# A two-block transformer kernel: second projection's chunks in another order, the gate's turn later, and splits, turns and squares moved at the handovers

## The reference

```python
# first block
h = rms_norm(x, g)
proj = h @ w_in            # 8708 columns: q, k, v of four kinds of attention, forget logits, gates
x = x + sum(sigmoid(gate) * (ys @ w_branch)) @ w_out
h = rms_norm(x, g)
x = x + square(relu(h @ w_up)) @ w_down          # 4096 hidden
x = rms_norm(x, g)
# second block
h = rms_norm_2(x, g)
q, k, v, u = split(h @ w_in)                     # 512 + 512 + 512 + 1024 columns
q, k = rope(rms_norm(q)), rope(rms_norm(k))      # by head of 64
attn = moba_attention(q, k, v)
a, g = split(u + b)
conv = silu(layer_norm(depthwise_conv31(a * sigmoid(g)) + b))
x = x + concat(attn, conv) @ w_out
h = rms_norm_2(x, g)
x = x + (silu(h @ w_gate) * (h @ w_up)) @ w_down # 2816 hidden
```

## Time and profile before

| | us |
|---|---|
| three timed runs | 823.29, 818.70, 821.35 (median 821.35) |
| the profiled execution | 819.01 |
| its span | 817.2 |
| PE busy | 784.6 |
| DVE busy | 476.5 |
| ACT busy | 407.1 |
| POOL busy | 41.7 |

### The profile page before, as it was taken

One profiled execution on the slowest core, in us unless ns is written; L12 is line 12 of the kernel. 1 busy time (PEld: TensorE's weight loads), 2 busy tenths in 40 slices (PEclk: granted clock), 3 DMA queues, 4 the chain that ended last, 5 costly groups with the idle time before them and its releaser, 6 DMA issues.

```text
span 817.2 us, 9727 instructions
## 1 busy us (share of the span) xinstructions
PE 784.6 (96%) x3930; PEld 657.3 (80%) x3930; DVE 476.5 (58%) x623; ACT 407.1 (50%) x542; POOL 41.7 (5%) x38
## 2 busy tenths in 40 slices
PE   7999999999999899999999999898999999999997
PEld 5787889888888687888888877776887888888896
DVE  5555365657765867454445437788956644545443
ACT  6565455455656536455454545555455543343340
POOL 0200000000000400000000004011000000000000
PEclk9999999999999999999999999999999999999999
DMA  9842424434445355655655553845122755655341
GB/s 330 312 156 81 152 78 156 154 114 145 155 157 203 117 183 198 212 182 176 205 185 176 196 165 132 332 147 168 53 63 96 255 192 172 203 177 184 104 155 51
DMA packets 68508, 136.25 MB, mean 167 GB/s; under 512 B 2416, under 2 KB 7152, under 8 KB 67824
## 3 DMA queue, kind: packets, MB, share of 16 engines
q1 hardware_dynamic: 68000, 134.44, 48.3%
q10 hardware_dynamic: 464, 1.20, 0.4%
HBM read 134.43 MB, written 1.05 MB: 166 GB/s over the span
## 4 chain that ended last, share of the span: by engine, by line
PE 80%; DVE 10%; ACT 5%; issue 3%; POOL 1%; DMA 1%; ACTq 0%; SPq 0%; DVEq 0%; POOLq 0%
PE b L573 18%; PE b L575 18%; PE b L574 18%; PE SS L573 4%; PE SS L574 4%; PE SS L575 4%; PE TT L542 3%; DVE ca L1913 2%; DVE wlo L1457 2%; PE OO L575 2%; PE OO L574 2%; PE OO L573 2%; ACT whi L1035 2%; PE SS L656 1%; PE b L713 1%
## 5 line engine op out<-in xcount | busy, mean ns | idle before, releaser
L1457 DVE TENSOR_TENSOR wlo<-raw,whi 128x2048 fp32r<-128x2048 f32 (+2 forms) x123 | 273.9, 2229 | 165.0 <-ACT whi L1035 164.8
L1035 ACT CAST whi<-raw 128x2048 fp32r<-128x2048 f32 (+2 forms) x123 | 227.3, 1850 | 125.4 <-PE b L575 87.5
L573 PE MATMUL b<-whi,Ahi 128*128 128x512 f32 (+2 forms) x568 | 222.1, 391 | 4.3 <-DVE wlo L1457 1.8
L575 PE MATMUL b<-whi,Alo 128*128 128x512 f32 (+2 forms) x568 | 215.4, 379 | 0.0
L574 PE MATMUL b<-wlo,Ahi 128*128 128x512 f32 (+2 forms) x568 | 214.9, 378 | 0.0
L573 PEld LDWEIGHTS b<-whi,Ahi 128*128 128x128 f32 x568 | 107.3, 189 | 25.2 <-issue 2.6
L575 PEld LDWEIGHTS b<-whi,Alo 128*128 128x128 f32 x568 | 107.0, 188 | 20.7
L574 PEld LDWEIGHTS b<-wlo,Ahi 128*128 128x128 f32 x568 | 107.4, 189 | 18.2
L573 PE MATMUL b<-whi,Bhi 128*128 128x512 f32 x168 | 66.8, 398 | 2.7 <-DVE gates L1723 2.7
L575 PE MATMUL b<-whi,Blo 128*128 128x512 f32 x168 | 65.5, 390 | 0.0
L574 PE MATMUL b<-wlo,Bhi 128*128 128x512 f32 x168 | 65.5, 390 | 0.0
(11 more groups left out here) (270 smaller groups left out, 1003.7 us busy)
## 6 DMA issues: line engine op xcount, KB each, us to landing
raw<-in_w_in SPq DMA_DIRECT2D x40, 1024.0 KB, 4.9
raw<-in_w_up SPq DMA_DIRECT2D x16, 1024.0 KB, 5.4
raw<-in_w_dn SPq DMA_DIRECT2D x16, 1024.0 KB, 4.9
raw<-in_w_d SPq DMA_DIRECT2D x11, 1024.0 KB, 4.9
raw<-in_w_g SPq DMA_DIRECT2D x10, 1024.0 KB, 5.1
raw<-in_w_u SPq DMA_DIRECT2D x10, 1024.0 KB, 5.0
raw<-in_w_out SPq DMA_DIRECT2D x8, 1024.0 KB, 4.9
raw<-in_w_br SPq DMA_DIRECT2D x4, 1024.0 KB, 4.9
```

The costliest lines, as they stand in the source:

```text
L573: e.matmul(dst, xh, H[:, kc, c0:ce], start=first and kc == krs[0], stop=False)
L575: ins = e.matmul(dst, xl, H[:, kc, c0:ce], start=False, stop=last and kc == krs[-1])
L1035: e.copy(whi[:, s, 0:m], raw[:, r, 0:m]).then_inc(s_hi, 1)
L1457: e.tensor_tensor(wlo[:, s, 0:m], raw[:, r, 0:m], whi[:, s, 0:m].bitcast(F32), ALU.subtract).then_inc(s_lo, 1)
```

## The change

1. `CH2` becomes gate, q, k, convolution input, v. `evac2` puts the chunks where they were wanted; `ut` waits for chunk 3 instead of 1, `r0` and `ra` for chunks 1 and 2 instead of 2 and 3.
2. `timetable2` is written anew: the gate's turn two groups later, the work on q and k four slots earlier (tiles 2 and 3 also), the turn of the convolution's input eight slots later, the eight taps in slots 18 and 19.
3. Turns and splits of hidden tile 0 of both MLPs go behind the second group of the next tile (`last_h`, `last_g`); those of the last tile go behind the third group of the `down` before it.
4. In `gained` DVE's split of a unit goes between the gain and the subtraction (`between`), that is into the time in which ACT rounds.
5. At the start the squares change places with `input_hi(0, 1)`, pieces 3, 4, 5 and with the last rounding of x; the variance and lambda's sum go ahead of `split_lo(2)`.
6. The last `down` is four groups instead of two, and DVE adds each quarter as soon as it is there.

```diff
-CH2 = [(2048, 512), (1536, 512), (0, 512), (512, 512), (1024, 512)]
+CH2 = [(2048, 512), (0, 512), (512, 512), (1536, 512), (1024, 512)]
...
-    for i, (a, b, c) in enumerate(((11, 13, 15), (12, 14, 16), (15, 17, 18), (16, 18, 19))):
+    for i, (a, b, c) in enumerate(((7, 9, 11), (8, 10, 12), (11, 13, 14), (12, 14, 15))):
...
-    for s, n in ((10, 4), (11, 2), (13, 1), (14, 1)):
+    for s, n in ((18, 4), (19, 4)):
...
             u = add_unit(src, 4 * j, kn, 0, 1024)
             for t in range(2):
-                group(u, name, j, 0, t)
+                for n in range(2):
+                    group(u, name, j, n, t)
...
@@ PE @@
-            for c0 in range(0, n, 512):
+            for c0 in cols or (0,):
...
-            w.wait_ge(s_ev, 36 + (2 if c == 0 else 0) + i + 1)
+            w.wait_ge(s_ev, 36 + (6 if c == 0 else 0) + i + 1)
...
         for j in range(8):
-            up("up", j, "N1", Bhi, Blo, (lambda: turn_res("N1", 1, 1)) if j == 0 else None)
+            def turn_h(j=j):
+                for t in range(2):
+                    w.wait_ge(s_up, 2 * j + t + 1)
+                    turn_x(("H", j, t), ust[:, j % 2, t, :])
+
+            if j == 0:
+                up("up", 0, "N1", Bhi, Blo, lambda q: turn_res("N1", 1, 1) if q == 0 else None)
+            else:
+                up("up", j, "N1", Bhi, Blo, (lambda q: last_h() if q == 1 else None) if j == 1 else None)
+            last_h = turn_h
             gone[1], gone[2] = (s_up, 2 * j + 1), (s_up, 2 * j + 2)
             if j:
-                down("dn", j - 1, "H", False)
-            for t in range(2):
-                w.wait_ge(s_up, 2 * j + t + 1)
-                turn_x(("H", j, t), ust[:, j % 2, t, :])
+                down("dn", j - 1, "H", False, (lambda k: turn_h() if k == 2 else None) if j == 7 else None)
+            if 0 < j < 7:
+                turn_h()
...
@@ ACT, start @@
         piece_hi(0, 1)
         piece_hi(0, 2)
-        w.wait_ge(d_x00, 16)
-        w.wait_ge(d_x01, 16)
-        input_square(0)
         input_hi(0, 1)
         piece_hi(0, 3)
         piece_hi(1, 0)
         piece_hi(1, 1)
+        w.wait_ge(d_x00, 16)
+        w.wait_ge(d_x01, 16)
+        input_square(0)
         piece_hi(1, 2)
         input_hi(1, 0)
         piece_hi(1, 3)
+        w.wait_ge(d_x1, 16)
+        input_square(1)
         input_hi(1, 1)
         split_hi(2)
-        w.wait_ge(d_x1, 16)
-        input_square(1)
...
@@ DVE @@
-        split_lo(2)
-        w.wait_ge(d_par, 16)
         w.wait_ge(s_sq, 2)
         variance("r1", r1v, ss1, D)
+        w.wait_ge(d_par, 16)
...
         e.tensor_reduce(lamt, lscr.rearrange("p (a b) -> p a b", a=2), AX.X, ALU.add).then_inc(s_lam, 1)
+        split_lo(2)
...
             x_gain(key, col, dst)
+            if between:
+                between()
             x_lo(key, dst)
...
         for t in range(2):
-            w.wait_ge(s_mm, done("d2", 5, 0, t))
             for n in range(2):
+                w.wait_ge(s_mm, done("d2", 5, n, t))
                 residual(12, t, n)
```

129 lines of the change are left out of this document (84 added, 45 removed).

## The result

The changed kernel takes **816.76 us** (median of 6 runs, 816.5 to 817.5); the kernel before, timed beside it, 822.25 us (6 runs). The ratio is 0.9934, 95% interval 0.9911 to 0.9958, or 5.5 us less by the medians. The forecast was 814.0 from 820.4, a gain of 6.4.

The account below looks back on a forecast made before the run. PE was taken to bound the kernel, except DVE in the second block's attention. Gains of 1.2 (start), 3.8 (handovers), 0.6 (end) and 0.8 (second block) sum to 6.4, so 820.4 becomes 814.0 us; range 810.0 to 819.0.

Parts of the forecast that it names:

- the handovers: Both MLPs' first and last hidden tiles: turns covered by other matmuls no longer wait; gain 3.8 us, bounds 3.0 and 4.0.
- start: Kernel start: earlier variance and rounding let chunk 1 begin at 21.6 instead of 22.87; gain 1.2 us, bounds 0.3 and 1.7.
- first hidden tiles of the first MLP (j = 0): PE's turn waits at 323 to 325 us go, and relu is done earlier; gain 1.2 us.
- very end: Last product in four groups, DVE adding each quarter when ready, leaves one addition behind the last matmul; gain 0.6 us.
- second block, to the first maxima: From the second block's first projection to DVE's first maxima: gain only 0.8 us, 1.3 and 0.2 at the two ends.
- First wait of the projection: Second block's projection: PE's 1.76 us wait at 505.19 goes, as the split starts earlier and ends by 501.9.
- Second wait: PE's 2.09 us wait at 513.00 isn't removed by moving the gate's turn; slot 4 starts at 510.3 instead of 513.4.
- for ACT's eviction: Sign of being right: a wait of about 2 us at the second block's chunk 1 first product, ended by ACT's eviction.
- both walked ends: Slot 4 starts at 509.8 or 510.85, by whether POOL's multiplications or DVE's subtraction come first; nothing between.
- Third wait: The 3.27 us wait for rotated keys at 561.11 returns in slot 14, with the convolution's input work now behind it.
- the third that came: Sign: if DVE's first maximum comes later against the last down-projection, the moved convolution costs more than its places free.
- The clock rival: PE's clock falls to 1.2 GHz in slot 14 and stays low through slots 15 to 19: 828 us, chance 5%.

Follow-up runs that it names:

- e7: The changed kernel with twelve unused matmuls filling PE's 3.27 us wait in slot 14: 815.94 us, ratio 0.9911.
- e1: The changed kernel with the turns of q and k tiles 2 and 3 one slot later (15 and 16): 812.89 us, ratio 0.9885.
- e2: The changed kernel with the old chunk order and timetable, all other edits kept: 812.62 us, ratio 0.9887.
- e4: The changed kernel with DVE's split of a unit behind the subtraction again, as before: 820.02 us, ratio 0.9973.
- e6: e1 with twelve convolution taps in slot 18 instead of four each in slots 18 and 19: 811.32 us, ratio 0.9864.
- e8: The changed kernel with POOL's four multiplications of x cut from 512 columns to one each, computation incomplete: 814.10 us, ratio 0.9897.
- e9: e6 with six instead of seven taps per round of the second block's attention: 808.60 us, ratio 0.9856.
- e10: e9 with unused matmuls at two long PE waits, the ten at slot 4 waiting for the next unit's split first: 810.54 us, ratio 0.9880.
- e5: The kernel before with only the turns, roundings and subtractions of both MLPs' first and last hidden tiles moved: 818.63 us, ratio 0.9946.
- e11: The kernel before with unused matmuls at three long PE waits (nine, twelve and seven), waiting for the next unit's split first: 822.85 us, ratio 1.0019.
- e12: e9 with unused matmuls whose operands are ready, six and ten, inside its two long PE waits: 806.96 us, ratio 0.9819.

## Why the prediction was right or wrong

The direction and most of the mechanism held, the time (816.8 for 814.0) stands inside the range. That the gain came so near is in part luck: the second block fell 2.0 us short and the clock was not in the sum, while the handovers and the end brought 1.1 more than forecast, mostly through the split's new place, which was priced at nothing there. Point by point, after's own two clock stretches taken off:

| term | forecast | measured |
|---|---|---|
| start | 1.2 | 0.7 at chunk 1, 0.9 by chunk 2 |
| first hidden tiles of the first MLP (j = 0) | 1.2 | 1.6 |
| last of the first MLP | 1.2 | 1.2 |
| first of the second MLP | 0.5 | 1.0 |
| last of the second MLP | 0.9 | 0.8 |
| very end | 0.6 | 0.9 |
| second block, to the first maxima | +0.8 | **-1.2** |
| the clock | 0 | **-1.6**, twice |

**Start**: the mechanism held. The wait at 22.87 is gone, and the two waits that the walk put at 0.5 each measure 0.43 (14.71) and 0.23. The size can't be read from one pair of executions, since x lands at another time in each: PE's first turn is at 3.97 in after, 4.09 in before, 5.18 in e7. With the new start, chunk 1 begins at 21.61 to 21.92 in e1, e2, e4, e6, e8, e9 and e10 and at 22.17 in after, against 22.87 to 23.18 in before, e5 and e11. The forecast had 21.6.

**Handovers and end**: 4.6 in the trace of after for 3.8, above the upper bound of 4.0. But the handovers alone (e5) brought 3.4, less than the 3.8. The other 1.2 us are the split's new place: e4 loses 0.9 in the first tiles of the first MLP and 0.3 in those of the second when it is undone. The forecast saw that relu comes earlier by it and gave that no price. With the end it is 5.5 for 4.4.

**First wait of the projection**: it shrank to 0.46 and did not go. The failed step is "this wait goes": the split was indeed over in time (it began at 497.79), but the *subtraction*, which stands behind the split now, took 1.78 us beside POOL from 500.00 on, and PE waited for that. The walk had nothing for it. I had let POOL and DVE meet at one place, where they met before. When the split moves, they meet elsewhere: at 489.58, 492.31 and 500.00.

**Second wait**: "for ACT's eviction" was half right. The row names DVE's split of the next unit, ended at about 509.9; ACT's eviction of the first tile (begun at 509.01) ended a quarter of a microsecond earlier. Both hang on the same late gain of x. Slot 4 was forecast at 510.3 on before's clock, 25.4 behind the down-projection, and came 27.34 behind it. **This is the mis-sized term**: 1.9 us, and e8 puts it down to POOL (24.61 without its work). It also lies outside both walked ends (509.8 and 510.85, that is 24.9 and 26.0 behind the down-projection), of which the forecast said that there is nothing between them: it had let POOL and DVE meet once, and they met three times.

**Third wait**: right in place, length and cause (3.27 us for DVE's PT in slot 14; e1 removes it), and so was the chain behind it. From slot 4 to the first maxima the forecast's walk gives 566.0 - 510.3 = 55.7; measured are 57.4, less the 1.6 of the clock stretch 55.8. Of the outcomes named ahead it is the third that came: the first maxima are later against the last down-projection than before (84.71 for 81.92), 1.6 of that by the clock. And the forecast's conclusion was too kind. A reader of my own numbers could have asked what the old order would give with the same gains ahead of it. The answer (e2) is 2.3 us less at the same clock, and 4.1 by the medians: the old order had its transfers, mask copies and taps *ahead* of the late turn, and I only counted what the new order costs against the kernel before, as a whole, never the order against the rest of the change.

**The clock rival** (5%, 828) was the wrong size and the wrong kind. I reasoned that a wait of 3.3 us either drops the clock for five slots or not at all, and took one execution in which it did not as proof that it does not. What happens is in between: 3.41 us at the lower level, 1.6 us lost, in some executions and not in others. The row I cited against it (clock 1.00 at 561 to 567) was true of that execution alone. The Trainium skill (TensorE: Matmul & The Clock Gate, Part 1) has idling PE fall back to the lower level, as I had cited; e7 and e12 agree, filled waits stayed at 1.00. Here waits of 1.63 us were long enough to have a stretch behind them (e4, e6, e7, e8), about half of the 3.3 us that I had looked at.

**The base** was off for the same reason. The runs of before at a mean clock of 0.999 took 818.6 to 819.0, those at 0.991 to 0.994 took 822.6 to 826.2; the profiled execution was one of the first kind, and its 819.0 is no typical time. I split the difference (820.4) without knowing what it was. Before's median of 822.25 holds some 3 us of lower clock, after's about as much: the sum of gains at equal clock is about 5.2 (819.0 - 813.8, and e7's runs at clock 1.0 took 813.5 and 813.9), close to the 5.5 of the medians. The mean clock alone does not give a run's time, though: after took 816.8 at 0.998 and 816.5 to 817.5 at 0.994. Where a stretch falls and when x lands count too.

What stays open: why some long waits bring a stretch and others, as long, none; and how the gain divides in the runs that were timed without a profile, since only the profiled execution of each kernel can be taken apart.

## What to carry to other kernels

When an order is changed, price it against the rest of the change and not only against the kernel before: here the new order moved work from ahead of a late turn to behind it, and without it the rest of the change is 2.3 us faster at the same clock (4.1 by the medians). When an instruction is moved on an engine that shares a port with another, its collisions move with it, so look for the neighbour at the new place. Take a kernel's wait not only by its length but also by what the clock may do behind it, and compare the granted clock of each timed run before building a sum on one profile; a wait that can't be removed can be filled with unused matmuls, provided that their operands are ready when the wait begins.

## What the runs showed of the hardware

Of PE's waits of 1.6 us or more, the 14 profiles of this case hold 53. Eighteen stretches at a granted clock of 0.5 occur in them (those at the very end of a kernel left out), each 3.41 us long, and **all 18 begin between 0.53 us before and 1.44 us after the end of such a wait**. The other 35 waits have none. In e12, the one kernel without such a wait, there is none. A stretch costs 1.4 to 1.6 us where PE is the bound: e1 and e6, alike there but for a stretch from 507.84 in e6, start slot 4 at 508.10 and 508.06 and slot 8 at 520.01 and 521.46. In e4, e6, e7 and e8 one falls at the end of the second block's attention, and the product behind it stands 33.1 us behind the first maxima instead of 31.5. Where DVE is the bound it costs nothing (e4, 570.70). The mean clock of a timed run goes with their number, since one lowers it by 0.002 (half of 3.41 us in 815).

I had not expected either that POOL, busy for 5% of the time, would cost the kernel 2.7 us through four multiplications that nobody on PE waits for directly (e8).
